# Attention heads of a latent-attention block: the order of exponentials, copies, transposes and value products

## The reference, cut to what matters

```python
def causal_block_attention(q_nope, q_rope, k_nope, k_rope, v):
    scale = (QK_NOPE_DIM + QK_ROPE_DIM) ** -0.5
    def one_block(args):
        qn_b, qr_b, j = args
        qpos = j * Q_BLOCK + jnp.arange(Q_BLOCK)
        s = (jnp.einsum('bqhd,bkhd->bhqk', qn_b, k_nope)
             + jnp.einsum('bqhd,bkd->bhqk', qr_b, k_rope)).astype(jnp.float32) * scale
        s = jnp.where(kpos[None, :] <= qpos[:, None], s, -jnp.inf)
        p = jax.nn.softmax(s, axis=-1).astype(v.dtype)
        return jnp.einsum('bhqk,bkhd->bqhd', p, v)
```

## Time and profile before

| | us |
|---|---|
| median of 3 runs | 2791.85 (2791.53 to 2796.41) |
| the profiled execution, its own time | 2799.07 |
| span of the profiled execution | 2797.2 |
| units of the heads, in the trace | from about 1733 to 2113 |
| the output projection with routing | about 2113 to 2253 |
| the experts of the last layer | about 2253 to 2790 |

### The profile page before, as it was taken

How to read it: one execution, slowest core, us unless ns; L and a number is a source line. 1 busy time by engine, 2 the same in 40 slices (tenths; PEclk the granted TensorE clock), 3 DMA queues, 4 the chain that set the end, 5 groups by cost and what they waited for, 6 DMA issues and landing times. The chain is left out here.

```text
span 2797.2 us, 38759 instructions
## 1 busy us (share of the span) xinstructions
PE 2478.4 (89%) x16010; PEld 1527.8 (55%) x16010; DVE 1062.5 (38%) x2148; ACT 543.9 (19%) x1226; POOL 345.1 (12%) x365
## 2 busy tenths in 40 slices
PE   9999988889999898987777898889889989877776
PEld 5444567448888555544444465656555555444443
DVE  3473654675455653211111254445445432111113
ACT  1312555110000111111111231322221121111112
POOL 3321002400000311111111000000003111111110
PEclk9999999999999999999999999999999999999998
DMA  3011010220112237999999850000113399999998
GB/s 116 34 41 53 1 48 5 100 105 31 46 46 102 98 128 306 424 425 424 426 425 426 364 228 8 24 16 8 52 44 136 116 397 424 425 425 426 425 425 342
DMA packets 88723, 566.01 MB, mean 202 GB/s; under 512 B 19408, under 2 KB 19568, under 8 KB 59344
## 3 DMA queue, kind: packets, MB, share of 16 engines
q1 hardware_dynamic: 63504, 506.86, 44.3%
q0 software_dynamic: 20144, 38.79, 3.6%
q10 hardware_dynamic: 4896, 17.83, 1.6%
HBM read 529.06 MB, written 65.01 MB: 212 GB/s over the span
## 5 line engine op out<-in xcount | busy, mean ns | idle before, releaser
L3289 PE MATMUL ex__h_ps<-all__arena,ex__xT 128*64 128x256 f32 x3392 | 410.6, 397 | 107.3 <-DMA all__arena<-in_w_up_t 83.0
L3289 PEld LDWEIGHTS ex__h_ps<-all__arena,ex__xT 128*64 128x64 f32 x3392 | 251.2, 143 | 278.8 <-DMA all__arena<-in_w_up_t 122.5
L3340 DVE COPY ex__ysb<-ex__y_ps 128x512 f32<-128x512 f32 x64 | 44.3, 692 | 492.8 <-PE ex__y_ps L3309 482.8
L3309 PE MATMUL ex__y_ps<-b__w,ex__hT 128*64 128x512 f32 x640 | 148.7, 606 | 28.0 <-issue 28.0
L3469 POOL DMA_INDIRECT b__rows<-s_hn,mo__queue x60 | 60.6, 1010 | 745.9 <-PE ex__x_ps L3282 745.9
L3331 DVE TENSOR_TENSOR ex__hs<-ex__sg,ex__h_ps 128x256 f32<-128x256 f32 x64 | 27.0, 422 | 307.8 <-PE ex__h_ps L3289 307.8
L2534 PE MATMUL cm__acc<-all__arena,cw__w 128*128 128x260 f32 x576 | 136.0, 386 | 2.3 <-PEq L84 2.3
L2534 PE MATMUL cm__acc<-all__arena,cm__sums 128*128 128x260 f32 x576 | 134.9, 384 | 0.0
L2534 PEld LDWEIGHTS cm__acc<-all__arena,cw__w 128*128 128x128 f32 x576 | 110.4, 192 | 19.8 <-issue 2.7
L2534 PEld LDWEIGHTS cm__acc<-all__arena,cm__sums 128*128 128x128 f32 x576 | 110.1, 191 | 17.2
L3322 ACT COPY ex__xT<-ex__x_ps 128x512 f32<-128x512 f32 x64 | 37.5, 586 | 380.3 <-PE ex__x_ps L3282 380.3
(11 more groups left out here) (552 smaller groups left out, 4128.2 us busy)
## 6 DMA issues: line engine op xcount, KB each, us to landing
all__arena<-in_w_up_t SPq DMA_DIRECT2D x62, 2048.0 KB, 43.9
all__arena<-in_w_gate_t SPq DMA_DIRECT2D x40, 2048.0 KB, 43.7
b__w<-in_w_down_t SPq DMA_DIRECT2D x40, 2048.0 KB, 44.7
mo__wx<-in_w_gate_t SPq DMA_DIRECT2D x22, 2048.0 KB, 43.6
all__arena<-in_w_down_t SPq DMA_DIRECT2D x22, 1024.0 KB, 38.2
mo__wx<-in_w_down_t SPq DMA_DIRECT2D x20, 1024.0 KB, 44.2
all__arena<-s_ys SPq DMA_DIRECT2D x15, 1024.0 KB, 11.1
cw__w<-in_conv_w_in_t SPq DMA_DIRECT2D x24, 512.0 KB, 4.3
```

What stands on the lines that cost most here:

```text
L3289: last = nc.tensor.matmul(h_ps[half, c, DE * b:DE * b + DE], xT[:, b, k, half], slots[c][:, n, k], start=(k == 0), stop=(k == KT - 1))
L3309: last = nc.tensor.matmul(y_ps[half, c], hT[:, b, k, half], rows[k][:, n, 512 * c:512 * c + 512], start=(k == 0), stop=(k == 1))
L3340: return nc.vector.tensor_copy(ysb[:, b, 512:], y_ps[:, 1])
```

## The change

Two edits in `heads`. In `turns_and_mixes` (PE) each turn is issued ahead of the mix piece of the same step, where it was behind it. In ACT's loop, for odd `n` above 1 (`n` = 3, 5, 7), the exponentials of unit `n` head 1 are issued ahead of the copies of unit `n - 1` head 1; the other `n` keep their order. Odd units are the upper blocks of a pair of blocks that are mixed together. No instruction is added, removed or changed in size, no wait is written differently, and no transfer is moved.

```diff
@@ -2965,9 +2965,9 @@
                             turn(j, n, *group)
                         return
                     for g in range(QUADS[2 * m + 1]):
-                        mix(j, m, h, g)
                         if g < len(turns):
                             turn(j, n, *turns[g])
+                        mix(j, m, h, g)
 
                 for j in range(NPAIR):
                     if j == 0:
@@ -3038,8 +3038,11 @@
                         evacuate(j, n - 1, 0, range(QUADS[n - 1]))
                         evacuate(j, n - 1, 1, range(ahead))
                         exponentials(j, n, 0)
+                        if n % 2 and n > 1:
+                            exponentials(j, n, 1)
                         evacuate(j, n - 1, 1, range(ahead, QUADS[n - 1]))
-                        exponentials(j, n, 1)
+                        if n % 2 == 0 or n == 1:
+                            exponentials(j, n, 1)
                     for h in range(2):
                         evacuate(j, NB - 1, h, range(QUADS[NB - 1]))
```

## The result

The changed kernel takes 2772.6 us (median of 4, 2770.45 to 2773.04) beside 2792.31 us for the kernel before in the same series: a ratio of 0.9925 (that of the medians alone is 0.9929), 95% interval 0.9908 to 0.9942, 19.7 us less. In a second series it took 2773.53 beside 2798.29 us: 0.9908 (0.989 to 0.9925), 24.8 us less. Both intervals hold the forecast's 0.9922 (21.8 us).

A forecast was written before the change was run, and what follows sets the result against it. Heads are bound by PE and the DVE and ACT chain it awaits, experts by their weights. (1.70 + 1.05 + 1.69 + 0.78) x 4 = 20.9, plus 0.9, is 21.8 us off the 2791.85 median: 2770.1 us, range 2763 to 2781.

The forecast's parts named there:

- unit 3's scores: PE's wait ahead of them closes as turns precede mix pieces and ACT copies earlier: 1.70 us a pair (bounds 1.59, 1.74).
- unit 4's: PE's wait ahead of unit 4's scores closes with exponentials issued before copies on ACT: 1.69 us a pair.
- unit 5's: PE's wait ahead of unit 5's scores shrinks through earlier turns, ACT staying a little late: 1.05 us a pair (0.9 to 1.32).
- unit 5's transposes: PE's wait ahead of head 1's transposes closes with exponentials just behind their maxima: 0.78 us a pair.
- the last pair: Unit 7's wait of 1.11 us, with no projections to hide it, shrinks: 0.9 us gained (bounds nothing and 1.27).
- good signs: In the heads: L2903's waits for L3014 24.1 to about 8 us; L3112's 4.3 to about 1; pairs about 5 shorter.
- bad signs: Waits of L2933 for L3027, new waits for DVE's L3101 chain, or heads 22 us earlier with an unchanged end.
- the later mix: In units 3 and 5's intervals, a turn ahead makes the mix end some 0.1 us later, hidden.
- The clock: Slow clock at unit 2's nope products costs 5.9 us, left unchanged in the sum; bounds -5.9 to +4.8 us.
- The rival in which fewer gaps calm the clock: Clock stays up in all pairs of the heads: another 5.9 us gained, 2764.2 us; chance 0.12.
- Absorbed behind the heads: Experts' weights set the end from a fixed time, so the heads' saving is lost: 2791.9 us; chance 0.04.
- Late copies: Copies behind exponentials hold up turns ahead of units 3, 5 and 7: 9.5 us slower at most, 2801.4; chance 0.03.

The follow-up runs named there:

- the run with n = 4 split: Changed kernel, plus for n = 1, 2 and 4 head 1's exponentials ahead of the previous unit's head 1 copies except the first: 2759.3 us, 0.9854 of before.
- the swap alone: Kernel before with only PE's edit, each turn issued ahead of the mix piece, ACT's order unchanged: 2794.17 us beside 2799.0, ratio 0.9976.
- the reorder alone: Kernel before with only ACT's edit, head 1's exponentials ahead of copies for n = 3, 5, 7, PE's order unchanged: ratio 0.9955, 12.6 us less.

## Why the prediction was right

*The sum.* 21.8 us were forecast; the heads gave 24.36, of which 1.0 is clock, so 23.3. Pair by pair, from the distances in the table: unit 3's scores 1.80 for 1.70, unit 4's 1.77 for 1.69, unit 5's 1.23 for 1.05, unit 5's transposes 0.80 for 0.78 with 0.05 us beside it, all four times, and 0.73 us for the 0.9 of the last pair. No term had the wrong sign or place. The largest miss is unit 5. Its scores start 0.24 us behind PE's last work, for 0.25 reckoned, so ACT was read right; but PE's own work from unit 4's scores on takes 7.58 us, as the run with n = 4 split shows, where the earlier trace rows gave me 1892.06 - 1884.33 = 7.73. The same sort of difference, 0.06 to 0.08 us, is in units 3 and 4: work that follows without a wait is a little shorter than the same rows behind one. In the last pair a wait of 0.29 us for the copy moved behind the exponentials is left, the one place where the price of the reorder shows.

*The signs named.* Of the good signs, waits of L2903 for L3014 came to 7.0 us (about 8 was said), those for DVE's scaling to 0.7 (about 1), the copies still wait for L2949, and from pair to pair the heads are 5.6 us shorter by the table's distances (about 5). Two of the bad signs came as well, and small: the wait for a copy, and new waits for DVE's maxima. Those are ACT's (12 more), not PE's; the exponentials ahead of unit 4 were placed just behind their maxima in the forecast, so they belong to it.

*What hides the swap's cost.* I put the later mix at 0.1 us and hidden. In the changed kernel it is hidden; with the swap alone it is 0.24 us at unit 4 and 0.11 at unit 7, because there the exponentials stand behind the copies. The two edits help each other a little, which I had not said.

*The clock.* I left it unchanged in the sum, at 5.9 us by the lengths of unit 2's products (6.1 us by the distances), with bounds; it went to 5.1 us. The likeliest case was that, and it held, though not for a reason that the forecast had: with the swap alone the clock cost 9.2 us and with the reorder alone 3.4, so that both together stay near the cost of before is in part luck. The rival in which fewer gaps calm the clock failed for this change: 16 gaps closed and one narrowed, and again three of four pairs are slow. With the rule of the Trainium skill (TensorE: Matmul & The Clock Gate, on psum-queue depth-cycling) that short idles between groups make the clock swing, the traces agree only ahead of unit 2: closing the wait of 1.75 us gave full clock in all 12 pairs of three kernels, two with the smaller gaps closed and one with them open.

*Absorbed behind the heads.* 684.36 and 684.49 us behind the last mix settle this: all of it arrives at the end.

*Late copies.* Their stall exists (4.23 and 3.49 us), but for head 0's copies. Head 1's cost 0.29 us once, in the last pair.

*The median.* The first series' 19.7 us is less than the heads' 24.4. The second series gave 24.8. Where single executions of the kernel before gained on the profiled one was not shown; the intervals (16 to 26 and 21 to 31 us) both hold 23 to 24 us.

## What to carry to other kernels

On an engine that takes its work in order, look at what stands behind an instruction that waits: if its inputs are there and another engine will soon need its result, it belongs ahead. Then count for the moved one what the next engine needs of it and when; here head 1's copies had 0.9 us to spare at unit 3 and 0.1 at unit 5, and head 0's had none. A gap's price can be more than its length: the 1.9 us in front of unit 2 cost another 1.3 to 1.5 us a pair in clock, on average.

## What was not expected of the hardware

At unit 2, with waits of 1.44 and 1.75 us ahead of it, 0.77 us of transposes apart, the granted clock fell to 1.2 GHz in 3, 3, 3, 2, 3 and 4 of 4 pairs of the six kernels that have both (3 again when the changed kernel was repeated), and in none of 12 pairs of the three that lack the second. In the second pair of the kernel before it was down already at the end of the wait of 1.75 us (0.50 from 1858.50 to 1859.10). Single waits of 1.16 to 1.58 us left it at 2.4 GHz wherever they stood alone, in the kernel before and in the runs, and so did a single wait of 2.21 us ahead of unit 1 in the first pair, in all ten traces; in the run with the swap alone it fell once in four behind a single wait of 1.85 us. So the length of the last wait alone does not decide. That two waits close together add up would fit, and is not shown. Waits of 4.23 and 3.49 us brought it down every time. In the two profiles of the changed kernel it fell in the same pairs; what picks the pairs stays open.
